# Seven weight units of each convolution mixer multiplied in three fp32r products instead of one fp32 product

## The chip, the cores and the metric

One core of a Trainium2 chip runs the whole kernel in one launch. The metric is the device time of one execution in microseconds (us). The kernel before takes 1773.08 us, the median of three executions (1772.91 to 1773.47).

Engines are called PE (TensorE, the matrix engine), DVE (VectorE), ACT (ScalarE), POOL (GpSimd) and SP (SyncE, which here only issues DMAs).

## The reference

The reference is a stack of six layers over 256 tokens of width 1024. The change touches only the layer that occurs twice in the first half, the conformer convolution mixer. Cut to what matters:

```python
def conformer_conv_mixer(h, w_in, conv_w, conv_b, ln_g, ln_b, w_out):   # h: 256 x 1024, w_in: 1024 x 6144
    proj = h @ w_in
    val, glu_gate, z = jnp.split(proj, 3, axis=-1)                      # 2048 channels each
    u = val * jax.nn.sigmoid(glu_gate)
    u = causal_depthwise_conv(u, conv_w) + conv_b                       # 31 taps
    u = jax.nn.silu(layer_norm(u, ln_g, ln_b))                          # over the 2048 channels
    return (u * jax.nn.silu(z)) @ w_out

# order of layers: conformer (a0), forgetting attention (b), short convolution (c), conformer (a1),
# then twice: a token mixer (m0, m1) and a convolutional feed-forward net (f0, f1)
```

## The kernel before, in words

All inputs and outputs are fp32. The weights are streamed once, in 629 pieces of at most 128 partitions x 1024 elements (512 KB), in an order fixed by `plan` (L365). SP loads them in that order into a ring of six buffers (`raw`, NRAW). Piece i can be loaded only when piece i-6 has been released, and SP issues strictly in order (`load`, L422).

A piece is used in one of two ways.

- A **plain** piece is read by PE straight from `raw` as fp32 (`plain_unit`, L565): eight matmuls with a 128x128 weight and 256 columns, for each of which the trace has two records. The buffer is released when PE has finished the unit.
- A **split** piece is first cast by ACT into an upper part (`wh`, the copy L113, in `feed_act` L463), and DVE then writes the rest, raw minus upper part, into `wl` (the subtraction L120, in `feed_dve` L475; called the low below). PE then does three fp32r matmuls for each of the eight weights, 24 in all (`unit`, L515). The `raw` buffer is released when the cast and the low are done, before PE has used them. `wh` and `wl` are rings of five.

A unit is one piece of 128 output channels. In a conformer layer (`plan_a`, L202; one program per engine: `pe_a` L844, `act_a` L922, `dve_a` L1057, `pool_a` L1197) the 2048 channels are taken in eight pairs of units p = 0 to 7. For each p PE multiplies the gate units g{p}.0 and g{p}.1, then the value units v{p}.0 and v{p}.1, and at p = 2, 4 and 6 one unit of z. Before the change all g are plain, v0.0, v0.1 and every v{p}.1 are plain, and v1.0 to v7.0 are split. The z units 0 to 7 (z0 to z3) are plain, the others split.

From p on, the work goes like this:

1. ACT takes the sigmoid of g{p} (`gate`).
2. DVE multiplies it by the value pair (`val(p)`: TENSOR_TENSOR `B<-ps,tmp` 128x512). This needs v{p}.1 from PE.
3. The convolution of pair p has 31 taps. ACT makes the first two. DVE adds 17 or 18 into PSUM, each as two SCALAR_TENSOR_TENSOR (`ps<-B,C,ps`). The other 12 or 11 are scaled by ACT into a ring of three `tmp` buffers (ACTIVATE `tmp<-B,C`), and POOL adds each into SBUF by two TENSOR_TENSOR. The nested functions `item` and `items` give each engine its taps in one common order: `items(p, a, b)` runs places a to b-1 of 30.
4. `conv_end(p)` on DVE (TENSOR_TENSOR `B<-ps,B`) joins the two sums. ACT squares the result (`stats`), and PE sums it over channels (`stats(q)`, MATMUL `ps<-B,C` and `ps<-tmp,C`).

POOL has waits of its own (`let_low`, L1202): from place 21 of pair p on it waits until DVE has finished the low of v{p+2}.0.

After p = 7 PE goes through the remaining z units with stats(5), (6) and (7) between them, then the 16 pieces of the output projection. PE, ACT, DVE and POOL each run their program strictly in order. In a1, PE, ACT and DVE also carry steps of a bias table for a later layer.

Of the kernel before, what the change touches and what calls it, by code (L numbers as in the profile page):

```python
# [18 lines left out]
E = 2048  # L19
# [9 lines left out]
PLAIN_Z = 4  # L29
# [164 lines left out]
def tiles(name, layer, c0, n=128, kt=8):  # L194
    return [(name, layer, 128 * k, 128, c0, n) for k in range(kt)]
# [6 lines left out]
def plan_a(j):  # L202
    A, out = f"a{j}", []

    def two(kind, p, base, *how):
        for n in range(2):
            out.append((f"{A}.{kind}{p}.{n}", tiles("a_w_in", j, base + p * 256 + 128 * n), how[n]))

    def z_unit(x):
        return [(f"{A}.z{x // 2}.{x % 2}", tiles("a_w_in", j, 2 * E + x * 128), "plain" if x < 2 * PLAIN_Z else "split")]  # L210

    for p in range(8):
        two("g", p, E, "plain", "plain")
        two("v", p, 0, "split" if p else "plain", "plain")
        if p in EARLY_Z:
            out += z_unit(EARLY_Z.index(p))
    for x in range(len(EARLY_Z), 16):
        out += z_unit(x)
    for k in range(16):
        out.append((f"{A}.o{k}", [("a_w_out", j, 128 * k, 128, 0, D)], "split"))  # L220
    return out
# [154 lines left out]
class Net:  # L376
# [467 lines left out]
    def pe_a(self, pe, j):  # L844
        s, A = self.s, f"a{j}"
        XN = self.xn()
        if j == 0:
            self.pe_bias(pe, 0, 7)
        self.pe_entry(pe, A, self.xnt)
        bank, prior = self.a_order()  # L850
        U, V, Z = self.a_views()

        def pair(kind, p, units=(0, 1)):
            b = self.ps[bank[kind, p]]
            if j == 0 and p == 0 and kind == "z":
                pe.wait_ge(*s["evac"]["bias", 0])
            if (kind, p) in prior:
                k, q = prior[kind, p]
                pe.wait_ge(*(s["conv"] if k == "v" else s["evac"])[A, k, q])
            for n in units:  # L860
                o = b[:, n * T:n * T + T]
                if kind == "g" or (kind == "v" and (p == 0 or n == 1)) or (kind == "z" and p < PLAIN_Z):
                    self.plain_unit(pe, o, f"{A}.{kind}{p}.{n}", XN, A)
                else:
                    self.unit(pe, o, f"{A}.{kind}{p}.{n}", A)

        def stats(q):


            pe.wait_ge(*s["conv"][A, "done", q])  # L870
            pe.wait_ge(*s["square"][A, q])
            x = [V[:, 2 * q, :], V[:, 2 * q + 1, :], self.tmp[5][:, 0:T], self.tmp[5][:, T:2 * T]]
            for g in range(4):
                ins = pe.matmul(self.ps[2][32 * g:32 * g + 32, 0:T], self.c("ones", 0, 32), x[g], start=q == 0,
                                stop=q == 7)
            ins.then_inc(s["sums"].up((A, q)), 1)

        def table(p):
            if j and 1 <= p <= 5:
                self.pe_bias_turn(pe, p, 3)  # L880

        for p in range(8):
            pair("g", p)
            if j == 0 and p == 0:
                self.pe_bias_turn(pe, 0, 7)
            table(p)
            if p >= 3:
                stats(p - 3)
            pair("v", p)
            if j and p < 5:  # L890
                self.pe_bias(pe, p + 1, 3)
            if p in EARLY_Z:
                x = EARLY_Z.index(p)
                pair("z", x // 2, (x % 2,))
        pair("z", 1, (1,))
        stats(5)
        pair("z", 2)
        pair("z", 3, (0,))
        stats(6)
        pair("z", 3, (1,))  # L900
        pair("z", 4)
        pair("z", 5, (0,))
        stats(7)
        pair("z", 5, (1,))
        pe.wait_ge(*s["evac"][A, "S"])
        if j:
            pe.wait_ge(*s["evac"]["bias", 5])
        for b in range(2):
            ins = pe.matmul(self.ps[3][:, b:4:2], self.tmp[4][:, 128 * b:128 * b + 128], self.c("which", 0, 2), start=True,
                            stop=True)  # L910
        ins.then_inc(s["sums"].up((A, "tokens")), 1)
        pair("z", 6, (0,))
        pe.wait_ge(*s["norm"][(A, "m"), "root"])
        pe.wait_ge(*s["evac"][A, "z", 1])
        self.spread(pe, 7, self.m["sm"][:, 112:116], (A, "m"))
        pair("z", 6, (1,))
        pair("z", 7)
        for k in range(15):
            self.pe_out(pe, A, k, 16)
        self.pe_out_last(pe, A, [15])  # L920

    def act_a(self, act, j):  # L922
# [43 lines left out]
        def items(p, a, b):  # L966
            for n in range(a, b):
                item(p, n)
# [22 lines left out]
        self.feed_act(act, f"{A}.v1.0", 1)  # L991
        for p in range(8):
            items(p, 0, 4)
            if p == 7:
                self.feed_act(act, f"{A}.z4.1", 0)
            if j and p < 5:
                self.act_bias_out(act, p + 1, 3)
            items(p, 4, 10)
            if p < 7:
                gate(p + 1)  # L1000
                if j and p < 5:
                    self.act_bias(act, p + 1, 3)
            else:
                self.feed_act(act, f"{A}.z5.0", 0)
                silu_z(1)
            items(p, 10, 14)
            if p < 6:
                self.feed_act(act, f"{A}.v{p + 2}.0", 0)
            if p == 4:
                silu_z(0)  # L1010
            items(p, 14, 18)
            if p:
                stats(p - 1)
            if p == 7:
                self.feed_act(act, f"{A}.z5.1", 0)
            items(p, 18, 22)
            if p >= 6:
                self.feed_act(act, f"{A}.z4.0" if p == 6 else f"{A}.z6.0", 0)
            if p == 7:
                silu_z(2)  # L1020
            items(p, 22, 30)
# [35 lines left out]
    def dve_a(self, dve, j):  # L1057
# [37 lines left out]
        def conv_end(p):  # L1095
            o = V[:, 2 * p:2 * p + 2, :].rearrange("p a t -> p (a t)")
            for i in (2 * p, 2 * p + 1):
                dve.wait_ge(*s["conv"][A, "tap", i, steps[i]])
            dve.wait_ge(*s["poolconv"][A, 2 * sum(self.pool_taps(x) for x in range(p + 1)) - 1])
            dve.tt(o, self.ps[p % 2], o, ALU.add).then_inc(s["conv"].up((A, "done", p)), 1)  # L1100
# [12 lines left out]
        for p in range(8):  # L1113
            items(p, 0, 8)
            if p:
                conv_end(p - 1)
            if p == 7:
                self.feed_dve(dve, f"{A}.z4.1", 0)
            items(p, 8, 14)
            if p == 7:  # L1120
                self.feed_dve(dve, f"{A}.z5.0", 0)
            items(p, 14, 20)
            if p < 7:
                val(p + 1)
            if p < 6:
                self.feed_dve(dve, f"{A}.v{p + 2}.0", 0)
            if p == 7:
                self.feed_dve(dve, f"{A}.z5.1", 0)
            items(p, 20, 28)
            if p >= 6:  # L1130
                self.feed_dve(dve, f"{A}.z4.0" if p == 6 else f"{A}.z6.0", 0)
            items(p, 28, 30)
# [64 lines left out]
    def pool_a(self, pool, j):  # L1197
        s, A = self.s, f"a{j}"
        U, V, Z = self.a_views()
        n = 0  # L1200

        def let_low(p, item):  # L1202

            names = [f"v{p + 2}.0" if item >= 21 and p < 6 else None]
            if p == 7:
                names = [u for at, u in ((9, "z4.1"), (15, "z5.0"), (21, "z5.1")) if item >= at]
            for u in names:
                if u is not None:
                    pool.wait_ge(*s["low"][self.at[f"{A}.{u}"]])

        for p in range(8):
            before = {2 * p: None, 2 * p + 1: None}
            for item, k in enumerate(self.taps(p), 1):
                if k >= self.pool_taps(p):
                    continue
                let_low(p, item)
                sh, q = 30 - k, self.tmp[2 + n % 3]
                for i in (2 * p, 2 * p + 1):
                    h = (i % 2) * T
                    pool.wait_ge(*s["tap"][A, i, k])  # L1220
                    if before[i] is not None:
                        pool.wait_ge(*s["poolconv"][A, "t", i, before[i]])
                    pool.tt(V[:, i, sh:T], V[:, i, sh:T], q[:, h + sh:h + T], ALU.add).then_inc(
                        s["poolconv"].up((A, "t", i, k), (A, 2 * n + i % 2)), 1)
                    before[i] = k
                n += 1
# [1690 lines left out]
```

## Time and profile before

| | |
|---|---|
| three executions | 1772.91, 1773.08, 1773.47 us |
| the profiled execution, its own time | 1773.47 us |
| its span (first to last instruction) | 1771.7 us |
| PE busy | 1726.1 us (97%), clock 0.994 of full speed |
| DVE, ACT, POOL busy | 1454.9 us (82%), 1082.4 us (61%), 291.8 us (16%) |
| PE, fp32r with `XS,wh` / `XS,wl` | 3600 matmuls / 2120 matmuls |
| PE, plain fp32 (`B,raw`) | 1056 records, 235.5 us |
| DVE, the lows (`wl<-raw,wh`) | 467, mean 1242 ns |
| ACT, the casts (`wh<-raw`) | 467, mean 1045 ns |

The shares are averages over stages that differ. Layer a0 stands between 14 and 227 us of the span, layer a1 between 746 and about 965 us. The convolution loops, which the change touches, are a part of each. In the timelines a row is a run of like instructions, with its start, its length, their number, and in brackets how long the engine had been idle before and what ended it. Rows of neighbours overlap slightly: an instruction's length includes the part that runs beside its successor.

### The profile page before, as it was taken

Reading aid. Unit: us, or ns where it says so; the run is one execution under the profiler, and the core shown is the slowest. Engines: PE = TensorE matmul, PEld = TensorE weight load, DVE = VectorE, ACT = ScalarE, POOL = GpSimd, SP = SyncE. Lnnn points to the kernel's source line nnn. Section 1 sums busy time; section 2 is a strip of 40 time slices with the busy share of each in tenths; the row PEclk is TensorE's granted clock in tenths of the full one; section 3 lists DMA queues with packets and bytes.
Section 4 is the critical chain, followed back from the end, with each engine's and each line's share of the span. In section 5 each row is a group of like instructions: output and inputs, shape, how many; then the busy total and the mean of one; then the engine's idle time right before and its main releaser. Section 6 shows DMA issues by size and latency. Waiting matters only on the chain.

```text
span 1771.7 us, 29474 instructions
## 1 busy us (share of the span) xinstructions
PE 1726.1 (97%) x10858; PEld 1530.7 (86%) x10858; DVE 1454.9 (82%) x2797; ACT 1082.4 (61%) x2101; POOL 291.8 (16%) x396
## 2 busy tenths in 40 slices
PE   7999999999999999999999999999999999999997
PEld 6888888888889999988888989988888998988885
DVE  6998878877788888779977698779987688789887
ACT  6887665655464444478875556576566556566664
POOL 2996000000000000068930000002000200002000
PEclk9999999999999999999999999999999999999998
DMA  6554568855568888644455664546774544546662
GB/s 224 154 163 159 168 217 306 266 183 178 183 211 290 289 291 295 215 143 143 143 179 167 202 202 121 173 147 190 243 230 157 167 145 129 176 139 189 222 191 71
DMA packets 92735, 339.53 MB, mean 192 GB/s; under 512 B 10288, under 2 KB 10672, under 8 KB 91952
## 3 DMA queue, kind: packets, MB, share of 16 engines
q1 hardware_dynamic: 92592, 337.64, 58.3%
q8 instruction: 87, 1.43, 0.3%
q14 instruction: 56, 0.46, 0.1%
HBM read 336.55 MB, written 1.05 MB: 191 GB/s over the span
## 4 chain that ended last, share of the span: by engine, by line
PE 79%; DVE 12%; ACT 7%; issue 1%; DMA 1%; SPq 0%; ACTq 0%; DVEq 0%
PE ps L104 78%; DVE wl L120 4%; ACT tmp L110 3%; ACT wh L113 2%; PE ps L107 2%; DVE tmp L130 1%; DVE raw L130 1%; DVE tmp L120 1%; DVE sm L142 1%; ACT os L113 1%; DVE tmp L125 1%; DVE B L120 0%; DVE os L120 0%; DMA raw<-in_w 0%; DVE sc L151 0%
## 5 line engine op out<-in xcount | busy, mean ns | idle before, releaser
L104 PE MATMUL ps<-XS,wh 128*128 128x256 f32 (+1 forms) x3600 | 773.3, 306 | 9.1 <-DVE wl L120 4.9
L120 DVE TENSOR_TENSOR wl<-raw,wh 128x1024 fp32r<-128x1024 f32 x467 | 571.8, 1242 | 107.6 <-ACT wh L113 105.5
L104 PEld LDWEIGHTS ps<-XS,wh 128*128 128x128 f32 x3600 | 577.3, 190 | 48.8 <-issue 18.5
L104 PE MATMUL ps<-XS,wl 128*128 128x256 f32 x2120 | 583.7, 281 | 0.0
L113 ACT CAST wh<-raw 128x1024 fp32r<-128x1024 f32 x467 | 473.9, 1045 | 154.2 <-PE ps L104 140.3
L104 PEld LDWEIGHTS ps<-XS,wl 128*128 128x128 f32 x2120 | 403.1, 190 | 6.6
L120 POOL TENSOR_TENSOR B<-B,tmp 128x236 f32<-128x236 f32 (+11 forms) x368 | 249.6, 717 | 652.9 <-ACT tmp L110 641.4
L104 PE MATMUL ps<-wh,os 128*128 128x512 f32 x864 | 280.7, 393 | 3.1 <-DVE B L133 2.1
L104 PE MATMUL ps<-B,raw 128*128 128x256 f32 x1056 | 235.5, 383 | 0.0
L104 PEld LDWEIGHTS ps<-B,raw 128*128 128x128 f32 x1056 | 200.4, 192 | 31.0 <-issue 4.4
L130 DVE SCALAR_TENSOR_TENSOR ps<-B,C,ps 128x253 f32<-128x253 f32 (+17 forms) x560 | 216.9, 475 | 3.8 <-ACT ps L110 3.8
L104 PEld LDWEIGHTS ps<-wh,os 128*128 128x128 f32 x864 | 163.1, 189 | 36.6 <-issue 3.8
L104 PE MATMUL ps<-wh,XS 128*128 128x512 f32 x576 | 179.5, 391 | 0.0
L104 PE MATMUL ps<-wl,os 128*128 128x512 f32 x432 | 169.0, 391 | 0.0
L110 ACT ACTIVATE tmp<-B,C 128x236 f32<-128x236 f32 (+11 forms) x368 | 151.4, 477 | 25.3 <-POOL B L120 24.6
L120 POOL TENSOR_TENSOR X<-X,B 128x512 f32<-128x512 f32 x24 | 42.1, 1753 | 701.9 <-PE ps L104 701.9
L110 ACT ACTIVATE B<-ps 128x256 f32<-128x256 f32 (+2 forms) x156 | 72.9, 480 | 117.4 <-PE ps L104 117.1
L104 PEld LDWEIGHTS ps<-wh,XS 128*128 128x128 f32 x576 | 107.2, 188 | 21.5
L110 ACT ACTIVATE tmp<-ps 128x128 f32<-128x128 f32 (+3 forms) x178 | 73.3, 427 | 80.5 <-PE ps L104 64.0
L130 DVE SCALAR_TENSOR_TENSOR raw<-raw,cb 128x1024 f32<-128x1024 f32 x96 | 116.5, 1219 | 0.0
L104 PE MATMUL ps<-wl,XS 128*128 128x512 f32 x288 | 112.3, 390 | 0.0
L104 PEld LDWEIGHTS ps<-wl,os 128*128 128x128 f32 x432 | 81.6, 189 | 16.2
(162 smaller groups left out, 1636.6 us busy)
## 6 DMA issues: line engine op xcount, KB each, us to landing
raw<-in_w SPq DMA_DIRECT2D x628, 512.0 KB, 4.4
B<-in_ln SPq DMA_DIRECT2D x4, 1024.0 KB, 6.6
C<-in_cst SPq DMA_DIRECT2D x1, 1103.5 KB, 9.9
X<-in_x SPq DMA_DIRECT2D x2, 512.0 KB, 5.7
out_x<-X SPq DMA_DIRECT2D x4, 256.0 KB, 2.5
cb<-in_cb SPq DMA_DIRECT2D x1, 512.0 KB, 12.9
pos<-in_pos SPq DMA_DIRECT2D x1, 160.0 KB, 2.3
raw<-in_w SPq DMA_DIRECT2D x1, 128.0 KB, 2.0
```

The costliest lines, as they stand in the source:

```text
L104: return NOTHING if self.e is None else self.e.matmul(*a, **k)
L107: return NOTHING if self.e is None else self.e.transpose(*a)
L110: return NOTHING if self.e is None else self.e.activation(*a, **k)
L113: return NOTHING if self.e is None else self.e.copy(*a)
L120: return NOTHING if self.e is None else self.e.tensor_tensor(o, a, b, op)
L125: return self.e.tensor_scalar(o, a, s1, s2, op0) if op1 is None else self.e.tensor_scalar(o, a, s1, s2, op0, op1)
L130: return self.e.scalar_tensor_tensor(out=o, in0=a, scalar=s, in1=b, op0=op0, op1=op1, **k)
L142: return NOTHING if self.e is None else self.e.tensor_reduce(o, a, AX, ALU.max)
```

## The change

The seven units v1.1 to v7.1 of each conformer layer become split instead of plain, 14 units in all. So ACT casts and DVE subtracts for them, in places given by hand:

- v1.1 right after v1.0, ahead of the loop (by the lookahead of 1 that stands there already);
- v{p+1}.1, for p = 1 to 6, on ACT after place 3 of pair p, and on DVE after conv_end(p-1), which follows place 7 of pair p;
- POOL waits, from place 9 of pair p on, for that low.

```diff
-    def two(kind, p, base, *how):
+    def two(kind, p, base, how):
         for n in range(2):
-            out.append((f"{A}.{kind}{p}.{n}", tiles("a_w_in", j, base + p * 256 + 128 * n), how[n]))
+            out.append((f"{A}.{kind}{p}.{n}", tiles("a_w_in", j, base + p * 256 + 128 * n), how))
...
-        two("g", p, E, "plain", "plain")
-        two("v", p, 0, "split" if p else "plain", "plain")
+        two("g", p, E, "plain")
+        two("v", p, 0, "split" if p else "plain")
...
-                if kind == "g" or (kind == "v" and (p == 0 or n == 1)) or (kind == "z" and p < PLAIN_Z):
+                if kind == "g" or (kind, p) == ("v", 0) or (kind == "z" and p < PLAIN_Z):
                     self.plain_unit(pe, o, f"{A}.{kind}{p}.{n}", XN, A)
...                                                     # act_a
             items(p, 0, 4)
+            if 1 <= p < 7:
+                self.feed_act(act, f"{A}.v{p + 1}.1", 0)
...                                                     # dve_a
             if p:
                 conv_end(p - 1)
+            if 1 <= p < 7:
+                self.feed_dve(dve, f"{A}.v{p + 1}.1", 0)
...                                                     # pool_a, let_low
-            names = [f"v{p + 2}.0" if item >= 21 and p < 6 else None]
+            names = [f"v{p + 1}.1" if item >= 9 and 1 <= p < 7 else None, f"v{p + 2}.0" if item >= 21 and p < 6 else None]
```

On DVE, in a0, this is what now stands at p = 1, behind conv_end(0) (`B<-ps,B`). Each tap is a SCALAR_TENSOR_TENSOR; x2 is one tap for the two units of a pair:

```order
 L130 SCALAR_TENSOR_TENSOR ps<-B,C,ps 128x251 x2
 L120 TENSOR_TENSOR B<-ps,B 128x512
+L120 TENSOR_TENSOR wl<-raw,wh 128x1024
 L130 SCALAR_TENSOR_TENSOR ps<-B,C,ps 128x250 x2
 L130 SCALAR_TENSOR_TENSOR ps<-B,C,ps 128x249 x2
```

One low (of v2.1) has come in; the same stands at p = 2 to 6 and in a1, nothing else moves on DVE there.

On ACT, at the start of pair p = 1 of a0, the cast comes in behind the first tap that is meant for POOL. The casts write to the ring `wh`; the taps write to the ring tmp2, tmp3, tmp4:

```order
 L110 ACTIVATE B1<-B3,C 128x256 x2
 L110 ACTIVATE tmp2<-B3,C 128x236 x2
+L113 CAST wh1<-raw5 128x1024
 L110 ACTIVATE tmp3<-B3,C 128x235 x2
 L110 ACTIVATE tmp4<-B3,C 128x234 x2
```

Every later tap that ACT makes for POOL stands one cast further back.

On SP, the loads behind those of pairs p = 4 to 7 and of the plain z units of a0, each with what it waits for. Before:

```order
L154 DMA raw<-in_w 128x1024 [waits s_gemm] x3
L154 DMA raw<-in_w 128x1024 [waits s_low,s_cast]
L154 DMA raw<-in_w 128x1024 [waits s_gemm] x4
L154 DMA raw<-in_w 128x1024 [waits s_low,s_cast]
L154 DMA raw<-in_w 128x1024 [waits s_gemm] x6
```

And now:

```order
L154 DMA raw<-in_w 128x1024 [waits s_gemm] x2
L154 DMA raw<-in_w 128x1024 [waits s_low,s_cast] x2
L154 DMA raw<-in_w 128x1024 [waits s_gemm] x3
L154 DMA raw<-in_w 128x1024 [waits s_low,s_cast] x2
L154 DMA raw<-in_w 128x1024 [waits s_gemm] x5
```

A buffer that held v{p}.1 is now released by its cast and low instead of by PE's matmuls. The load that follows v7.1 in its buffer is that of z4.0, the first split unit of z.

## Rows read from the trace of the kernel before

**Rows 1.** Two windows: PE, PEld, DVE, ACT, POOL busy us (instructions), PEclk, DMA.

```profile
30.00:138.00 108.00, 108.00 (x600) 94.43 (x599) 104.11 (x251) 91.69 (x220) 98.74 (x154) 1.00 0.50 153
752.00:875.00 123.00, 123.00 (x716) 104.53 (x715) 105.60 (x253) 97.08 (x232) 101.04 (x154) 1.00 0.47 144
```

**Rows 2.** Chain of waits, a0: start us, us, what.

```profile
117.89 18.11 PE ps L104 x99
...
136.02 3.73 DMA raw<-in_w
```

**Rows 3.** Timeline of PE, a0: start us, us, instructions, idle before.

```profile
38.78 10.53 PE L104 MATMUL ps<-B,raw 128*128 128x256 f32 x48
...
154.06 0.41 PE L104 MATMUL ps<-B,C 128*32 128x256 f32 x2 [3.49 <-ACT tmp L110]
...
154.86 5.13 PE L104 MATMUL ps<-B,raw 128*128 128x256 f32 x16
159.64 0.59 PE L104 MATMUL ps<-XS,wh 128*128 128x256 f32 x2
...
168.55 0.41 PE L104 MATMUL ps<-B,C 128*32 128x256 f32 x2
```

**Rows 4.** Timeline of DVE, a0.

```profile
42.44 0.69 DVE L120 TENSOR_TENSOR B<-ps,tmp 128x512 f32<-128x512 f32 x1 [2.60 <-PE ps L104]
43.04 1.22 DVE L120 TENSOR_TENSOR wl<-raw,wh 128x1024 fp32r<-128x1024 f32 x1
44.18 7.71 DVE L130 SCALAR_TENSOR_TENSOR ps<-B,C,ps 128x243 f32<-128x243 f32 x20
...
52.38 6.21 DVE L130 SCALAR_TENSOR_TENSOR ps<-B,C,ps 128x250 f32<-128x250 f32 x16
58.48 0.70 DVE L120 TENSOR_TENSOR B<-ps,tmp 128x512 f32<-128x512 f32 x1
...
137.98 0.69 DVE L120 TENSOR_TENSOR B<-ps,tmp 128x512 f32<-128x512 f32 x1
...
165.03 0.69 DVE L120 TENSOR_TENSOR B<-ps,B 128x512 f32<-128x512 f32 x1 [1.18 <-POOL B L120]
```

**Rows 5.** Groups by form, DVE, 42.4 to 138 us: busy us, mean ns.

```profile
L120 DVE TENSOR_TENSOR wl<-raw,wh 128x1024 fp32r<-128x1024 f32 x6 | 8.9, 1479 | 0.0
```

**Rows 6.** The same for 775.5 to 862 us.

```profile
L120 DVE TENSOR_TENSOR wl<-raw,wh 128x1024 fp32r<-128x1024 f32 x6 | 8.2, 1370 | 0.0
```

**Rows 7.** DVE's waits, 776 to 875 us: total us, times, longest.

```profile
DVE B L120 <- PE ps L104: 4.9, 2, 2.8
```

**Rows 8.** Timeline of DVE, a1.

```profile
775.00 0.69 DVE L120 TENSOR_TENSOR B<-ps,tmp 128x512 f32<-128x512 f32 x1 [4.00 <-PE ps L104]
...
859.48 2.03 DVE L120 TENSOR_TENSOR wl<-raw,wh 128x1024 fp32r<-128x1024 f32 x1
...
874.97 0.69 DVE L120 TENSOR_TENSOR B<-ps,tmp 128x512 f32<-128x512 f32 x1
```

**Rows 9.** Timeline of POOL, a0 and a1.

```profile
124.59 15.31 POOL L120 TENSOR_TENSOR B<-B,tmp 128x228 f32<-128x228 f32 x24 [1.16 <-DVE wl L120]
...
861.59 15.30 POOL L120 TENSOR_TENSOR B<-B,tmp 128x228 f32<-128x228 f32 x24 [1.17 <-DVE wl L120]
```

**Rows 10.** Timeline of ACT, a0 and a1.

```profile
139.78 1.04 ACT L113 CAST wh<-raw 128x1024 fp32r<-128x1024 f32 x1 [2.76 <-DMA raw<-in_w]
...
142.99 0.15 ACT L110 ACTIVATE ps<-C 128x1 f32<-128x1 f32 x1
...
877.73 1.04 ACT L113 CAST wh<-raw 128x1024 fp32r<-128x1024 f32 x1 [3.72 <-DMA raw<-in_w]
...
880.95 0.15 ACT L110 ACTIVATE ps<-C 128x1 f32<-128x1 f32 x1
```

**Rows 11.** Timeline of PE after the stage between.

```profile
392.95 0.48 PE L104 MATMUL ps<-wh,os 128*128 128x512 f32 x1 [2.09 <-DVE B L133]
```

**Rows 12.** The window after it: busy us by engine, PEclk, DMA.

```profile
394.00:396.00 2.00, 2.00 (x6) 1.52 (x5) 0.89 (x1) 0.00 (x0) 0.00 (x0) 0.50 0.61 131
```

## The prediction, made before the changed kernel ran

> **What bounds the kernel now.** I read the busy time by windows first, then the chain of waits through layer a0, then the timelines of the four engines, side by side, for a0 and a1. The windows [rows 1] show two full engines. In a0's loop, 30 to 138 us, PE is busy 108 of 108 us, and DVE 104.1 with its only pauses at the start; POOL has 98.7 and ACT 91.7. In a1 PE is again full (123 of 123), while DVE has 105.6. So whatever a change takes from PE there, it must not hand to DVE.
>
> The chain in a0 [rows 2] runs on PE until 136.02, when v7.1 and with it its buffer is done. It then goes through the load of z4.0 into that buffer (3.73 us) and ACT's cast of it. From there it runs along ACT to the square for stats(6), which PE has waited 3.49 us for at 154.06 [rows 3]. After that PE runs on without a gap into the output projection. So the time of a layer hangs on when stats(6) can start.
>
> On DVE [rows 4] val(1) waits 2.60 us for PE at 42.44. After that no row has an idle time up to val(7) at 137.98, 95.54 us later. In a1 the same stretch takes from 775.00 to 874.97 [rows 8], 99.97 us, of which 4.9 us in two pieces are waits for PE [rows 7]. DVE's own work in it is 95.1 us. In a0 DVE sets the pace of the loop with PE just ahead of it; in a1 PE is in front in half of the pairs.
>
> **What PE gains.** Three plain units take 10.53 us [rows 3], 3.5 each. Three split units (z4.0, z4.1, z5.0) lie between 159.64 and 168.55 [rows 3], 2.97 each. So PE saves 0.5 to 0.6 us a unit, 14 x 0.55 = 7.7 us in both layers, if PE is what everything waits for. Only v1.1 is surely such a place: val(1) waits for it in both layers, and its low is made before val(0), where DVE in a1 is idle. I take -0.6 us for it in each layer.
>
> **What DVE pays.** Six lows per layer come between conv_end(p-1) and place 8 of pair p. A low is shown as 1.22 us, and 43.04 to 44.18 is 1.14 to the next start [rows 4]; the shown length holds 0.08 of overlap. The six lows in a0's loop average 1479 ns, the six in a1's 1370 [rows 5, 6]. Without the overlap that is 1.40 and 1.29 us. The longest is 2.03 [rows 8], so 1.95. The long ones are those that begin while POOL is adding. The new lows fall where POOL is in the midst of its adds, like most old ones, so I take these means; the bounds are 1.14 and 1.95.
>
> The Trainium skill (SBUF — State Buffer, section "SBUF: two separate sides") says that DVE, with two SBUF inputs, and GpSimd take a shared port pair as an exclusive lock for a whole instruction. By that rule a low would begin up to one POOL add late, and POOL would stand still during every low. The rows agree: POOL's runs of 24 begin with a wait of 1.16 us for a low [rows 9]. A run is 15.31 us, 0.64 an add, so a low that finds POOL in an add would cost up to 1.14 + 0.64 = 1.8 us by the rule; six of them make 10.7 us, inside my bounds.
>
> **POOL** loses about 1.16 us more per pair, as much as DVE. Its 24 adds (22 in every second pair) are 15.3 and 14.0 us. With two such waits that is 17.0 us a pair on average. DVE's pair becomes 15.9 + 1.4 = 17.3. So POOL keeps up, with little to spare. **ACT** pays six casts of about 1 us. It is busy 91.7 of 108 us [rows 1], and its cast comes some 2 us before DVE wants it; but its next tap for POOL is one cast later. I cost this at nothing; if POOL waits for it in each pair, some 0.5 us a pair are added.
>
> **When PE waits.** The new v{p+1}.1 can't start before its low. In p = 1 that ends at 52.38 + 1.4 - 0.6 = 53.2 us, and PE, done with v2.0 at about 51.3, waits 1.9. From the low to val(p+1) DVE has 14 or 16 taps before it, 58.48 - 52.38 = 6.1 us for 16 and 5.4 for 14 [rows 4]. PE's unit of 2.9 us fits in twice over. So these waits, up to 3.5 us each in a0 as DVE falls back, cost nothing by themselves. They only mean that PE's saving is not used. If PE's clock falls to half behind one of them, the unit takes up to 5.8 us, which fits 16 taps and just misses 14.
>
> **Sum for a0.** val(7) comes -0.6 + 6 x 1.40 = +7.8 us later, at 145.8. The low of v7.1 is done 14 taps earlier, at 140.4, and releases the buffer. The load takes 3.73 us, to 144.1. ACT wants z4.0 at 139.78 - 2.76 = 137.02, now + 7.8 = 144.8 [rows 10]. So ACT's wait for this DMA goes. What is late next is POOL: ACT's last tap of p = 6 needs the add with which POOL's run ends, 124.59 + 15.31 = 139.90 [rows 9], and with 0.8 us for the tap ACT would start pair 7 at 140.8 instead of 142.99 [rows 10]. The gain is 2.2 us, not 2.76. stats(6) moves by +7.8 - 2.2 = +5.6 us, to 159.7. PE arrives there at: 140.4 + 2.9 for v7.1, then 14.5 us as before (136.02 to 154.06 less 3.49), so 157.8, and waits 1.9 us. Behind it stats(7) must not be late. conv_end(7) is at 165.03 now, 1.18 us of that for POOL [rows 4]; DVE gets there at 163.85 + 7.8 = 171.7. Add 1.4 us for it and the square: 173.1, and PE comes at 168.55 + 5.6 = 174.2 [rows 3]. It holds by 1.1 us.
>
> **Sum for a1.** DVE has 95.1 + 6 x 1.29 = 102.8 us of work from val(1), which starts at 775.0 - 0.6 = 774.4. So val(7) is at 877.2 instead of 874.97, +2.2: most of the new lows fill what were waits for PE. PE, now 0.55 us a unit faster, is not in front any more. ACT starts pair 7 at 880.95; without the wait of 3.72 us for the DMA it would be POOL's end, 861.59 + 15.30 + 0.8 = 877.7 [rows 9, 10], 3.2 us earlier. stats(6) moves by 2.2 - 3.2 = -1.0 us.
>
> **Total:** +5.6 - 1.0 = +4.6 us. Between a0 and a1 and behind a1 nothing is changed, and PE is the engine that runs through there, so both shifts are carried to the end. The profiled execution took 1773.47 us (span 1771.7 and 1.8 around it), which makes 1778.1. It is the slowest of the three; against the median of 1773.08 the forecast is 1777.7 us.
>
> **Bounds.** With lows of 1.14 us a0 has -0.6 + 6.8 - 2.2 = +4.0, a1 1.3 - 3.2 = -1.9, together +2.1. PE's clock may add a gain: the unit after the 3.49 us wait took 5.13 us instead of 3.5 [rows 3], and after a wait of 2.09 us the granted clock was 0.50 too [rows 11, 12], the lower of the two levels (1.2 of 2.4 GHz). The new waits for stats(6) are 1.9 us, so I count on no gain (nearest row 2.09). If the clock stays up it is up to 1.3 us a layer: +2.1 - 2.6 = -0.5, or 1772.6. With lows of 1.95 us it is +8.9 and +2.9, together +11.8: 1784.9.
>
> **Rivals.**
> - *PE is the bound, and it is faster.* PE is full in both loops [rows 1]. Then all 14 units pay, -7.7 us: 1765. Against it: in a0 DVE has no idle time from 42 to 138 us, and each of its pairs gets longer. A half of it could hold in a1, where DVE waits 4.9 us: with clean lows, the DMA wait gone and the clock up the two layers reach -0.5 us, not -3.5. I give 0.10 to faster.
> - *The new waits and the freed buffer balance.* Clean lows (1.14) and a clock that stays up, or PE's waits shorter than I think: +0 to +3 us, 1773 to 1776. For it: the first low in a0 is 1.14 [rows 4], and without the one of 2.03 the other five in a1 average (8.2 - 2.03) / 5 = 1.23, overlap included [rows 6, 8]. 0.25.
> - *POOL or ACT becomes the bound of the loop (slower by more).* POOL's adds and two waits come to 17.0 us a pair, and ACT's tap one cast later adds up to 0.5 us, 17.5 against DVE's 17.3. Then ACT, which waits for POOL's ring of three, doesn't get its 2.2 and 3.2 us back: 4.6 + 5.4 = +10.0, 1783. It decides as soon as POOL's pair is over 17.3 us. 0.20.
> - My forecast, +3 to +8 us: 0.45.
>
> Within 0.2% (3.5 us) this kernel's time can't be told from no change. The forecast of +4.6 lies a little over that. Slower by over 0.2% holds most of my own case and all of the POOL case, 0.65; within 0.2% gets 0.25, faster 0.10. The range leaves out the PE case and the far end of the slow ones: 1771 to 1785.
>
> **What would show it.** In the profile after, val(2) to val(7) in a0 stand 16.7 to 17.8 us apart (now 15.3 to 16.4), with one more `wl` row in each pair, and DVE without idle time from val(1) on. The PE rows have a wait for DVE `wl` before the second value unit of each pair in a0, at most 4 us; in a1 short ones or none. ACT has no wait for `raw<-in_w` before the cast of z4.0 in either layer. PE's wait for ACT before stats(6) is about 2 us. PE's busy time falls by some 7 us while the span grows. It is wrong if a0's DVE still shows 95 us from val(1) to val(7), which would mean that the lows found a gap, or if the stretch from stats(6) to the projection grows, which would mean that stats(7) or a z low is late.

## The result, and the profile after

The changed kernel takes 1783.69 us (median of four executions, 1781.24 to 1784.35), the kernel before 1773.28 in the same series. Over all nine executions on record (1781.24 to 1785.77) the ratio is 1.0055, interval 1.0042 to 1.0069. By the medians that is 10.4 us slower, by the ratio 9.8, where 4.6 were forecast. The profiled execution took 1785.77 us (span 1783.9), 12.3 more than that of before.

The page, busy us of each engine over the span:

```profile
PE 1725.5 (97%) x10970; PEld 1534.5 (86%) x10970; DVE 1480.0 (83%) x2811; ACT 1095.5 (61%) x2115; POOL 298.0 (17%) x396
```

Fourteen units are now cheaper on PE, and still its busy time is the same to 0.6 us. What went up is DVE, by 25 us. Two windows, one for the loop of each layer, show why [rows 1]; the columns are as there:

```profile
43.00:147.00 104.00, 96.16 (x580) 85.28 (x579) 103.73 (x235) 87.11 (x201) 92.33 (x139) 0.97 0.44 137
783.00:886.00 103.00, 98.58 (x631) 85.39 (x628) 102.14 (x232) 88.29 (x205) 95.57 (x136) 0.98 0.43 139
```

DVE is now the full engine in both layers, 103.7 of 104 us and 102.1 of 103. PE has 8 and 4 us of holes, and its granted clock is 0.97 and 0.98 instead of 1.00. So its work is less, but part of it runs at the lower level (0.57 in the window 88 to 96 us, 0.70 in 826 to 831). The lower level in these two windows costs about 0.03 x 104 + 0.02 x 103 = 5 us of PE time, an estimate, and takes up most of the 7 us by which PE's busy time was to fall.

The chain of waits through the same loop in a0 (start us, us, what), which ran on PE before [rows 2]:

```profile
43.10 0.69 DVE B L120
43.79 1.36 DVE wl L120
45.15 3.84 DVE ps L130 x11
...
52.77 0.59 DVE B L120
53.37 1.27 DVE wl L120
54.63 5.43 DVE ps L130 x15
...
147.54 3.77 DVE ps L130 x10
151.31 0.16 DVE wl L120
151.47 3.95 issue
155.42 3.94 DVE ps L130 x10
```

Each pair has two lows (`wl`), as forecast. The new thing is at the end, in pair 7: a low that begins at 151.31 is followed by 3.95 us of "issue". The timeline of DVE shows it as one long instruction, the low of z4.0, in a0 and in a1 (start us, us, instructions, idle before):

```profile
52.69 0.68 DVE L120 TENSOR_TENSOR B<-ps,B 128x512 f32<-128x512 f32 x1
53.29 1.34 DVE L120 TENSOR_TENSOR wl<-raw,wh 128x1024 fp32r<-128x1024 f32 x1
...
146.86 0.68 DVE L120 TENSOR_TENSOR B<-ps,tmp 128x512 f32<-128x512 f32 x1
147.47 3.84 DVE L130 SCALAR_TENSOR_TENSOR ps<-B,C,ps 128x243 f32<-128x243 f32 x10
151.22 4.27 DVE L120 TENSOR_TENSOR wl<-raw,wh 128x1024 fp32r<-128x1024 f32 x1
155.42 3.94 DVE L130 SCALAR_TENSOR_TENSOR ps<-B,C,ps 128x238 f32<-128x238 f32 x10
...
891.22 4.28 DVE L120 TENSOR_TENSOR wl<-raw,wh 128x1024 fp32r<-128x1024 f32 x1
```

From val(1), at 43.10 in the chain, to val(7) it is 103.76 us in a0 (95.54 before [rows 4]) and 104.51 in a1 (99.97 [rows 8]). The new low of pair 1 takes 1.34 us. The one of z4.0 takes 4.27 and 4.28; the longest of all others in these layers is 2.36. In the kernel before it was this:

```profile
142.33 1.33 DVE L120 TENSOR_TENSOR wl<-raw,wh 128x1024 fp32r<-128x1024 f32 x1
```

What POOL does in that time, after:

```profile
141.67 16.29 POOL L120 TENSOR_TENSOR B<-B,tmp 128x234 f32<-128x234 f32 x24 [1.65 <-DVE wl L120]
```

And before:

```profile
141.29 9.62 POOL L120 TENSOR_TENSOR B<-B,tmp 128x228 f32<-128x228 f32 x12 [1.39 <-ACT tmp L110]
```

Before, POOL idled 1.39 us for ACT, which was held up by the load of z4.0, and then did 12 adds in 9.62 us. One could read 0.80 us an add into this, and gaps between them; but record by record each add starts about 0.04 us before the last one ends, as after the change. Ten of them take about 0.67 us, and two take 1.65 and 1.67, because a low runs beside each. The first of the two, in the window 142.6 to 144.1 us:

```profile
L120 POOL TENSOR_TENSOR B<-B,tmp 128x227 f32<-128x227 f32 x1 | 1.6, 1649 | 0.0
```

The low at 142.33 began 0.25 us before the end of an add, got in at that end, and held up the next one. (In a1 before, the low began at 879.32, just after POOL had come out of an idle time of 2.35 us, and took 1.22 us.) After the change the low begins at 151.22, together with an add of POOL, and waits for this add and four more, to 154.41. So POOL's adds are no closer than before. What is new is that this low did not get in at the end of the first add. ACT is no longer held up there, and low and adds meet at another moment.

PE in the same places [rows 3] (timeline, start us, us, idle before); the first four rows are of a0, the last three of a1:

```profile
89.21 0.77 PE L104 MATMUL ps<-XS,wh 128*128 128x256 f32 x2 [3.43 <-DVE wl L120]
...
161.92 0.41 PE L104 MATMUL ps<-B,C 128*32 128x256 f32 x2 [2.50 <-DVE ps L130]
...
162.49 5.41 PE L104 MATMUL ps<-B,raw 128*128 128x256 f32 x16
...
176.88 0.41 PE L104 MATMUL ps<-B,C 128*32 128x256 f32 x2 [0.36 <-ACT tmp L110]
...
901.85 0.41 PE L104 MATMUL ps<-B,C 128*32 128x256 f32 x2 [2.41 <-ACT tmp L110]
...
902.41 3.72 PE L104 MATMUL ps<-B,raw 128*128 128x256 f32 x16
...
916.92 0.41 PE L104 MATMUL ps<-B,C 128*32 128x256 f32 x2 [2.15 <-ACT tmp L110]
```

Two kinds of waits are new. PE waits for a low five times in a0 (7.8 us together, the longest shown), which costs nothing by itself. And in a1 stats(7) at 916.92 is 2.15 us late; before, PE came there without a wait. The windows of 40 us behind stats(6) show the granted clock, the last but two of the columns, at 0.96 in both layers of the kernel after:

```profile
162.00:202.00 40.00, 39.64 (x275) 36.22 (x275) 33.73 (x64) 26.87 (x46) 11.46 (x15) 0.96 0.54 176
902.00:942.00 40.00, 37.85 (x268) 35.20 (x262) 32.58 (x62) 25.16 (x43) 11.48 (x15) 0.96 0.54 175
```

It was 0.96 before as well, so the change loses nothing there by the clock:

```profile
154.00:194.00 40.00, 39.94 (x276) 36.45 (x277) 30.62 (x58) 27.13 (x46) 10.89 (x14) 0.96 0.52 172
892.00:932.00 40.00, 39.99 (x278) 36.35 (x279) 30.27 (x56) 27.34 (x46) 10.91 (x14) 0.96 0.52 172
```

In a0 it fell behind the wait for stats(6), where 16 records took 5.41 us. In a1 these took 3.72, the time at the higher level (2.4 GHz), so it fell later, behind the wait for stats(7).

ACT in a0: the cast of z4.0, without the wait of 2.76 us [rows 10], its start of pair 7, and the cast of z5.0:

```profile
146.39 1.03 ACT L113 CAST wh<-raw 128x1024 fp32r<-128x1024 f32 x1
...
150.19 0.15 ACT L110 ACTIVATE ps<-C 128x1 f32<-128x1 f32 x1
...
153.85 1.63 ACT L110 ACTIVATE tmp<-B,C 128x235 f32<-128x235 f32 x4
156.04 1.05 ACT L113 CAST wh<-raw 128x1024 fp32r<-128x1024 f32 x1 [0.55 <-DMA raw<-in_w]
```

With this the two layers can be accounted for by stretch. a0 begins at PE's first x64 run of plain matmuls (22.09 us before, 23.34 after), a1 at the 16 short matmuls just ahead of that run (744.55 and 752.48). Each ends where PE starts the next layer. The column e1 is the first experiment below. Differences to before, us:

| stretch | before | forecast | after | e1 |
|---|---|---|---|---|
| a0: start to val(1) | 20.35 | -0.6 | -0.59 | -0.58 |
| val(1) to val(7) | 95.54 | +8.4 | +8.22 | +7.57 |
| val(7) to stats(6) | 16.08 | -2.2 | -1.02 | -1.05 |
| stats(6) to layer b | 77.94 | 0 | +0.46 | -1.64 |
| a1: start to val(1) | 30.45 | -0.6 | -0.58 | -0.59 |
| val(1) to val(7) | 99.97 | +2.8 | +4.54 | +3.93 |
| val(7) to stats(6) | 17.04 | -3.2 | -2.05 | -1.95 |
| stats(6) to layer m0 | 78.38 | 0 | +2.29 | -1.43 |
| sum | | +4.6 | +11.3 | +4.3 |

The profile of after also starts its first layer 1.25 us later than that of before. Experiments 3, 5 and 7 have it at 23.76, 23.13 and 23.36 us, 7 with a time like that of before, so I take it for spread.

### The profile page after: what moved, and what is told of

The parts are those of the page before. It is cut to its first block, busy times and chain, and to the rows that moved or that the text cites. A ratio compares the mean times of both kernels' runs of the same rounds, so it can differ in the third digit from the quotient of the medians.

```text
span 1783.9 us, 29766 instructions
## 1 busy us (share of the span) xinstructions
PE 1725.5 (97%) x10970; PEld 1534.5 (86%) x10970; DVE 1480.0 (83%) x2811; ACT 1095.5 (61%) x2115; POOL 298.0 (17%) x396
## 3 DMA queue, kind: packets, MB, share of 16 engines
HBM read 336.55 MB, written 1.05 MB: 189 GB/s over the span
## 4 chain that ended last, share of the span: by engine, by line
PE 69%; DVE 21%; ACT 7%; issue 2%; POOL 0%; DMA 0%; SPq 0%; ACTq 0%; DVEq 0%; POOLq 0%
PE ps L104 68%; DVE ps L130 7%; DVE wl L120 6%; ACT tmp L110 3%; ACT wh L113 2%; PE ps L107 2%; DVE B L120 1%; DVE tmp L130 1%; DVE raw L130 1%; DVE tmp L120 1%; DVE sm L142 1%; ACT os L113 1%; DVE tmp L125 1%; DVE os L120 0%; POOL B L120 0%
## 5 line engine op out<-in xcount | busy, mean ns | idle before, releaser
L104 PE MATMUL ps<-XS,wh 128*128 128x256 f32 (+2 forms) x3824 | 818.7, 306 | 18.3 <-DVE wl L120 14.1
L120 DVE TENSOR_TENSOR wl<-raw,wh 128x1024 fp32r<-128x1024 f32 x481 | 597.1, 1258 | 105.1 <-ACT wh L113 103.0
L104 PEld LDWEIGHTS ps<-XS,wh 128*128 128x128 f32 (+1 forms) x3824 | 615.8, 192 | 59.5 <-issue 29.3
L104 PE MATMUL ps<-XS,wl 128*128 128x256 f32 x2232 | 617.5, 282 | 0.0
L113 ACT CAST wh<-raw 128x1024 fp32r<-128x1024 f32 x481 | 488.1, 1044 | 145.1 <-PE ps L104 141.3
L104 PEld LDWEIGHTS ps<-XS,wl 128*128 128x128 f32 x2232 | 426.7, 191 | 6.6
L120 POOL TENSOR_TENSOR B<-B,tmp 128x236 f32<-128x236 f32 (+11 forms) x368 | 254.8, 730 | 659.8 <-ACT tmp L110 637.1
L104 PE MATMUL ps<-B,raw 128*128 128x256 f32 x832 | 186.8, 384 | 0.0
L104 PEld LDWEIGHTS ps<-B,raw 128*128 128x128 f32 x832 | 158.5, 193 | 24.9 <-issue 3.3
## 6 DMA issues: line engine op xcount, KB each, us to landing
C<-in_cst SPq DMA_DIRECT2D x1, 1103.5 KB, 10.4
```

The lines of the kernel that those rows point to most:

```text
L104: return NOTHING if self.e is None else self.e.matmul(*a, **k)
L113: return NOTHING if self.e is None else self.e.copy(*a)
L120: return NOTHING if self.e is None else self.e.tensor_tensor(o, a, b, op)
```

## The experiments

My theory: DVE's added lows are the price (near 5 us), and the rest of the 10.4 is the low of z4.0, shut out by POOL's adds. The rivals: POOL's new waits cost it, or PE's later clock, or the change costs by itself whatever z4.0 does. Later the question was whether the freed buffer or PE's saving can be had for less. All are compared with the kernel before on the same chip, at 1773.8 to 1774.4 us in these series. The executions of one kernel differ, and with them the granted clock. In experiment 4 the four executions with a granted clock of 0.996 took 1772.65 to 1773.14 us, those with 0.992 and 0.993 took 1777.88 to 1779.24. Several use a set `SECOND` of (layer, pair), which says for which v{p}.1 the change is made:

```diff
-        two("v", p, 0, "split" if p else "plain")
+        two("v", p, 0, "split" if p else "plain", "split" if (j, p) in SECOND else "plain")
...                                  # and in act_a, dve_a and let_low
-            if 1 <= p < 7:
+            if 1 <= p < 7 and (j, p + 1) in SECOND:
```

**1. POOL waits for z4.0's low.** The changed kernel, and in `let_low`:

```diff
+            if p == 6 and item >= 27:
+                names.append("z4.0")
```

> The changed kernel, and POOL also waits, from place 27 of pair 6 on, until DVE has finished the low of z4.0. Theory A (starved low): in the changed kernel the low of z4.0 is shown as 4.3 us in both layers instead of 1.3 because POOL's adds run back to back through it; this is on the path to stats(6). Then the row falls to 1.2 to 1.7 us, conv_end(6) comes 2.6 to 3 us earlier in each layer, and the time goes from 1783.7 to 1777 to 1780. Theory B (the long row is only overlap, the loss is the six lows in the loop alone): the row may shorten but the time stays at 1783 to 1785.

Measured: 1778.5 us (six executions), ratio 1.0033 (1.0021 to 1.0045). Its DVE timeline, a0:

```profile
145.79 0.67 DVE L120 TENSOR_TENSOR B<-ps,tmp 128x512 f32<-128x512 f32 x1
...
150.15 1.21 DVE L120 TENSOR_TENSOR wl<-raw,wh 128x1024 fp32r<-128x1024 f32 x1
...
155.13 0.67 DVE L120 TENSOR_TENSOR B<-ps,B 128x512 f32<-128x512 f32 x1
```

The low is 1.21 us again (1.75 in a1), and conv_end(6) comes 9.34 us after val(7) instead of 12.41. By the medians one wait on POOL takes back 5.2 us of the 10.4; by the ratios it is 3.9 of 9.8, and the two intervals just touch (1.0042 and 1.0045). So two fifths to a half of the slowdown was this one instruction per layer. The table shows by which way: stats(6) itself moves by little (0.7 and 0.5 us), but behind it the loss is 2.1 and 3.7 us. PE there:

```profile
160.82 0.41 PE L104 MATMUL ps<-B,C 128*32 128x256 f32 x2 [2.49 <-ACT tmp L110]
...
161.39 3.72 PE L104 MATMUL ps<-B,raw 128*128 128x256 f32 x16
```

stats(7) is not waited for any more in either layer, and the granted clock stays up:

```profile
162.00:202.00 40.00, 40.00 (x280) 37.04 (x279) 33.58 (x61) 27.36 (x48) 9.72 (x12) 1.00 0.57 185
```

**2. Meant to leave out the added lows.** A test of the units' names in my edit matched none of them, so all lows were still made; what ran is the changed kernel without POOL's new waits, and the expectation speaks of a kernel that did not run:

```diff
-            names = [f"v{p + 1}.1" if item >= 9 and 1 <= p < 7 else None, f"v{p + 2}.0" if item >= 21 and p < 6 else None]
+            names = [f"v{p + 2}.0" if item >= 21 and p < 6 else None]
```

> The changed kernel without the seven added lows of each layer (and without POOL's waits for them): ACT casts, PE does its three products with the upper part in place of the rest, so the small term of these units is left out. Theory A (DVE's lows are the price): val(1) to val(7) in a0 is back at 95 to 96 us and in a1 at 95 to 97, ACT's wait for the DMA of z4.0 is gone, and the kernel is faster than before: 1764 to 1769. Rival C (ACT's casts in front of POOL's taps, or PE's extra waits, are the price): the loop stays at 99 us or more in a0 and the time is 1774 or more.

Measured: 1790.63 us (1781.48 to 1799.79), ratio 1.009 (1.0064 to 1.0117). The miss shows something all the same. Its timeline in a0, POOL, DVE and PE:

```profile
62.09 14.04 POOL L120 TENSOR_TENSOR B<-B,tmp 128x228 f32<-128x228 f32 x22 [1.16 <-DVE wl L120]
...
70.13 7.08 DVE L120 TENSOR_TENSOR wl<-raw,wh 128x1024 fp32r<-128x1024 f32 x1
...
77.35 0.76 PE L104 MATMUL ps<-XS,wh 128*128 128x256 f32 x2 [6.10 <-DVE wl L120]
```

POOL's run of 22 adds ends at 62.09 + 14.04 = 76.13, and the low of v3.1, which should have begun at 70.13, ends at 77.21, 1.08 us behind that. It waited for the whole rest of the run, and PE 6.1 us for it. But it need not happen. In the same execution the low of v5.1 began just as long (0.30 us) before the end of an add, amid adds just as close, and got in at that end; POOL's add behind it is the long one. DVE, and POOL in the window 110.3 to 111.7 us:

```profile
109.93 1.39 DVE L120 TENSOR_TENSOR wl<-raw,wh 128x1024 fp32r<-128x1024 f32 x1
...
L120 POOL TENSOR_TENSOR B<-B,tmp 128x234 f32<-128x234 f32 x1 | 1.7, 1665 | 0.0
```

The six executions lie far apart. The fastest is as fast as the changed kernel's fastest, which would fit a number of shut-out lows that changes from one to the next; only one execution was profiled. So POOL's waits in `let_low` are no cost to be saved but what bounds the time of a low.

**3 and 4. One layer alone**: `SECOND` holds v1.1 to v7.1 of a0, or of a1.

> The change in layer a0 alone. Theory A: a0 carries 7 of the 10 us: 1779 to 1781.5, val(1) to val(7) in a0 103 to 104 us, z4.0's low 4.3 us there and 1.2 in a1. Theory D (a1 is where it is lost, since its PE and ACT carry the bias table as well): 1776 or less.

> The change in layer a1 alone. Theory A: a1 costs 3 to 4.5 us, of which 3 are z4.0's low: 1776 to 1778. My forecast for a1 (-1 us, without the starved low) would give 1772 to 1773. The shares of this run and of the one with a0 alone should add up to the whole, 10.4 us.

Measured: a0 alone 1780.36 us, ratio 1.0035 (1.0023 to 1.0047); a1 alone 1776.39, 1.0010 (1.0001 to 1.0018). That is +6.5 and +2.6 us, together 9.1 of the 10.4. The low of z4.0 follows the change: with a0 changed it is 4.29 us there and 1.21 in a1; with a1 changed it is 4.29 in a1. The layers add up within the spread, and a0, where DVE had no idle time, pays more, as forecast. The 2.6 us of a1 are the weaker number: the four executions with the highest granted clock were as fast as the kernel before.

**5. The added lows left out.** The kernel of 1, but DVE makes no low for v1.1 to v7.1, POOL waits for none, and PE multiplies these units with `wh` in place of `wl`. So the small term of the product is left out and the upper product is added twice; PE's and ACT's work is kept. Left out is each low together with POOL's wait for it, but experiment 2 shows that leaving out these waits alone gains nothing.

```diff
+    def no_low(self, i):
+        n = self.pieces[i][0]
+        return n[0] == "a" and n[3] == "v" and n[4] != "0" and n.endswith(".1")
...                                  # feed_dve
+            if self.kind[i] == "split" and self.no_low(i):
+                continue
```

> The changed kernel with POOL's wait for z4.0, and without the seven added lows of each layer and POOL's waits for them: ACT casts, PE does its three products with the upper part in place of the rest, so the small term of these units is left out. Theory A (the added lows on DVE are what the loop pays): val(1) to val(7) is 95 to 96 us in a0 and 95 to 97 in a1, the DMA wait before z4.0's cast is gone, stats(6) comes 2 to 4 us earlier than before in each layer, and the time is 1764 to 1769. Rival C (ACT's casts ahead of POOL's taps, or PE's new waits, are the price): the loops stay over 99 us in a0 and the time is 1773 or more.

Measured: 1768.41 us (1768.25 to 1768.8), ratio 0.9963 (0.9951 to 0.9976): 6.0 us faster than before, where 1 is 4.7 slower. Its lengths from val(1) to val(7) are 95.49 us in a0, the same as before, and 98.79 in a1. So the added lows are what makes the change slower, and PE's saving is there: 6.0 us, near the 7.7 of the forecast's PE rival. DVE's work in the loop takes it away. In a0 this kernel gains 2.0 us and in a1 4.3. In a0 DVE sets the pace even so; in a1 the granted clock also stayed at 1.00 over the 40 us behind stats(6), which was 0.96 before and is worth some 1.6 us. (The low of z4.0 was 2.26 and 2.90 us here in spite of the wait: POOL had still two and three adds to do before the place at which it waits.)

**6 to 8. Only the units at the ends of the loop**, where a low is cheap (v1.1's falls before val(0)) or buys something (v7.1's frees the buffer of z4.0). 6 is v1.1 and v7.1 in both layers with the wait of 1; 7 is v7.1 alone with it; 8 is v1.1 alone without it.

```diff
+SECOND = {(j, p) for j in range(2) for p in (1, 7)}     # 6; 7: (0, 7), (1, 7); 8: (0, 1), (1, 1)
```

> Only v1.1 and v7.1 of each layer are split, and POOL waits for z4.0's low. Theory A: v1.1 gains 0.6 us where DVE waits for PE; v7.1 costs one low (1.2 to 1.5 us in a0, less in a1 where DVE has waits) and releases z4.0's buffer early, worth 2.2 us in a0 and 3.2 in a1. Sum -1.5 to -2.8 in a0 and -3 to -4 in a1: 1767 to 1770, faster than both kernels. Rival E (stats(7) or POOL's end takes over at once, so the freed buffer is worth nothing): 1772.5 to 1775.

> Only v7.1 of each layer is split, and POOL waits for z4.0's low. Theory A: as the run with v1.1 and v7.1 but without the 0.6 us of v1.1 in each layer: 1768 to 1771. Rival E: 1773 to 1776.

> Only v1.1 of each layer is split; nothing else is changed. Theory A: val(1) comes 0.6 us earlier in each layer, and since the chain of waits runs on PE up to v7.1, the whole gains 0.5 to 1.2 us: 1772 to 1773. Rival F (the early low and cast delay val(0) and POOL, so nothing is gained): 1773.5 to 1774.5.

Measured: 1773.85, 1772.98 and 1773.44 us, against 1774.41: ratios 0.9996 (0.9987 to 1.0004), 0.9993 (0.9984 to 1.0002), 0.9995 (0.9986 to 1.0003). None can be told from no change, where 6 was expected at 1767 to 1770. In 6 ACT has no wait for z4.0, but 0.68 and 1.31 us for the load of z5.0 (0 before). The waits for the load after that one, 2.26 and 2.34 us, are hardly longer than before (2.24 and 2.10). So the freed buffer hands a part of its wait on to the next load.

**9 to 11. Four units of a1, one unit of a1, and the wait alone.**

```diff
+SECOND = {(1, 1), (1, 3), (1, 5), (1, 7)}               # 9; 10: (1, 7); 11: none. All with the wait of 1
```

> Layer a0 as before; in a1 only v1.1, v3.1, v5.1 and v7.1 are split, and POOL waits for z4.0's low. v1.1, v3.1 and v5.1 are the units for which DVE waited for PE in the kernel before (4.0, 2.1 and 2.8 us). Theory A (a low costs nothing where DVE would wait for PE, and full price elsewhere): val(1) to val(7) in a1 is 98 to 99.5 us, stats(6) comes 3 to 4 us earlier, a1 gains 3 to 4.5 us: 1769.5 to 1771.5. Rival E (the freed buffer and the loop gain nothing, since z5.0's load or stats(7) takes over): 1773 to 1775.

> Layer a0 as before; in a1 only v7.1 is split, and POOL waits for z4.0's low. The run with v7.1 in both layers gained 2.3 us in a1 by the marks in its profile and nothing in a0. Theory A: 1771 to 1772.5, of which the low of v7.1 takes back about 1.2 us of what the buffer gives. Rival E: 1773 to 1775.

> The kernel before with POOL's wait for z4.0's low alone, no further unit split. Theory A (that wait helps only where POOL has adds in hand while DVE wants the low; in the kernel before POOL was idle for 1.4 us there): 1773 to 1775, no difference that can be measured, z4.0's low 1.2 us in both layers. Rival G (the wait by itself speeds up or slows down the stage): more than 2 us away from before.

Measured: 1773.97, 1773.78 and 1773.88 us against 1773.87: ratios 1.0000 (0.9991 to 1.0009), 0.9998 (0.9989 to 1.0006) and 1.0001 (0.9992 to 1.0010). The wait alone does nothing, so 1 repaired what the change had broken and not a fault of before. 9 was to use a1's 4.9 us of idle DVE time [rows 7] and missed. From val(1) to val(7) it took 100.87 us, 0.9 more than before. Its PE and ACT:

```profile
891.17 0.41 PE L105 MATMUL ps<-B,C 128*32 128x256 f32 x2 [3.49 <-ACT tmp L111]
...
891.74 5.41 PE L105 MATMUL ps<-B,raw 128*128 128x256 f32 x16
```

```profile
885.29 1.05 ACT L114 CAST wh<-raw 128x1024 fp32r<-128x1024 f32 x1 [1.56 <-DMA raw<-in_w]
...
900.84 1.05 ACT L114 CAST wh<-raw 128x1024 fp32r<-128x1024 f32 x1 [2.34 <-DMA raw<-in_w]
```

The wait of 3.72 us for z4.0's load [rows 10] is gone; in its place z5.0 is waited for 1.56 us, and PE, which comes earlier, waits 3.49 us for stats(6) and runs the next 16 records at the lower level (5.41 us). The second wait, 2.34 us, was 2.10 before. No version with all products beats the kernel before by an amount that can be measured.

## Why the prediction was right, and where its size was off

It was right on direction (slower), on the range (1771 to 1785) and on the reason. Its steps, against the table:

- **v1.1 gains 0.6 us a layer.** Measured 0.58 to 0.59, four times.
- **Six lows in a0 cost 8.4 us.** 8.22 measured, 7.57 in 1. The new ones were 1.21 to 1.62 us (mean 1.32, 1.24 without the overlap), under my 1.40; the old low of pair 6 was 2.02. DVE is without idle time from val(1) on.
- **In a1 2.8 us.** 4.5 measured, 3.9 in 1. Too small: I took all of DVE's 4.9 us of waiting as room for lows. A wait for PE is left there (0.8 us at 852.48), and the twelve lows average 1.43 us, not 1.29 + 0.08.
- **The freed buffer gives 2.2 and 3.2 us.** Only 1.0 and 2.0. (139.90 + 0.8 is 140.7 and not 140.8, so the sum should have had 2.3.) The wait for z4.0 went, but ACT reached pair 7 not 2.2 but 1.7 us earlier in a0 (150.19 - 146.86 = 3.33 behind val(7), 5.01 before), and then waited 0.55 us for z5.0, whose load I had not followed.
- **Nothing behind stats(6).** This is where it failed. The prediction had: "Behind it stats(7) must not be late", and then "It holds by 1.1 us." It did not: 0.36 us late in a0, 2.15 in a1. The sum for conv_end(7) there had the low of z4.0 at its length of before. It took 3 us more, and in experiment 1, without these 3 us, stats(7) is in time. In a0 that is all of it: from stats(6) to stats(7) it is 14.96 us after and 12.86 in 1, which is the whole difference of 2.1 us between the two columns. The chain of waits runs on DVE there up to conv_end(7), so the fall of the clock behind stats(6) cost nothing more. In a1 it is 15.07 and 12.85, and the other 1.5 us of the 3.7 lie behind stats(7), where the clock fell (0.66 in the window 917 to 922 us).
- **PE's busy time falls by some 7 us** (a sign it named). It fell by 0.6: PE ran part of both loops at the lower level, as shown above.

That low is the mis-sized term. I priced the six new lows with bounds of 1.14 and 1.95 us, and moved the old ones at their old lengths. I had worked out that ACT's wait goes and that ACT and POOL then run closer, and did not ask how this low would meet POOL's adds. Its length was 4.27 us, outside the bound of 1.8 us that the prediction took for a low that finds POOL in an add. One sign was also misread: the 1.16 us in [rows 9] are POOL's own wait for the low in `let_low`. The row that shows DVE holding up POOL is the add of 1649 ns above.

The POOL rival (+10.0 us, 1783) met the time but not the way: POOL waits for lows 10.8 us in a0's loop and ACT still had its gain. It didn't decide the pace; it shut DVE out at one place.

With the low repaired, kernel 1 is 4.7 us over before by the medians (5.9 by the ratio), and 4.6 was forecast. The table says that this is partly luck. Against its column e1 the forecast is 3.5 us too low on three stretches (1.1 and 1.2 from val(7) to stats(6), 1.1 in a1's loop) and 0.8 us too high in a0's loop. It is also 3.1 us too high behind stats(6): that is the clock, whose gain of "up to 1.3 us a layer" I had put in the bounds and not in the sum. PE's waits for stats(6) were 2.49 and 2.53 us in 1, against 3.49 and 3.29 before, and the 16 records behind them took 3.72 instead of 5.13 and 4.70.

Two things stay open. Why the low of z4.0 missed the end of the first add, where most lows get in (last section), no profile tells; that a wait on POOL's side repairs it is shown. And the clock: it fell behind waits of 2.50 us (after, a0), 2.51 (experiment 10), 2.55 (7, a0) and 2.61 (6, a0), where the 16 records took 5.41 us. It didn't behind 2.49 and 2.53 (1), 2.55 (5, a1), 2.60 (3, a0) and 2.65 (2, a0), where they took 3.72. So the length of the wait alone does not decide it.

## What to carry to other kernels

Moving work from an engine that is full to one that is also full gained nothing here; look for the engine without idle time in the loop, and let it pay nothing (experiment 5: 6.0 us faster where the change is 10.4 slower). When a change removes a wait, follow every engine behind it: with ACT's wait for a DMA gone, an old DVE instruction met POOL's adds at another moment and took 3 us more. Where an instruction of DVE with both inputs in SBUF runs beside a busy POOL and the critical path goes through it, try a wait on POOL's side just ahead of it (4.27 to 1.21 us and 4.28 to 1.75 here); where it was short anyway the wait did nothing (experiment 11). And don't read a mean length of a row as gaps between its instructions: one long instruction among short ones gives the same mean.

## What the runs showed of the hardware

A DVE subtraction with both inputs in SBUF and an add of POOL do not run at the same time. In most cases the low gets in at the end of the add in whose course it begins. In the layers a0 and a1 of all 13 profiles, counted record by record, this was so 146 times. POOL's adds were back to back there (each began 0.03 to 0.07 us before the last one ended), the low was shown as 1.20 to 1.70 us, and the next add was the long one. In 27 cases the low missed this first end, and then it got in at no later end of an add either (25 more went by) until POOL stopped: at a wait or the end of its run 21 times, at a short pause 6 times. Most of the 27 met a wait of POOL after one more add and are 1.75 to 2.3 us long. The costly ones are those of z4.0 (4.27, 4.28, 4.29 and 4.29 us in three kernels, 4.05 in a1 of experiment 2) and of v3.1 (7.08 us, in a0 of experiment 2). What decides between the two cases the profiles don't tell: in experiment 2 two lows that began 0.30 us before the end of an add went different ways.

The pause that let the low of z4.0 in, in a0 of the changed kernel: one add ended at 154.41 us and the next began at 154.42, where all others of the run began 0.04 to 0.05 before the last one ended. That next add is shown as 1623 ns, where others of its form take about 680, in the window 154.9 to 155.8:

```profile
L120 POOL TENSOR_TENSOR B<-B,tmp 128x235 f32<-128x235 f32 x1 | 1.6, 1623 | 0.0
```

ACT's next taps for POOL begin at 153.85 us, behind a cast, so POOL had run out of taps about there. In the four other lows that got in so, the next add also began late, from 0.01 us before to 0.04 after the last one's end (0.23 in one more). That the pause is what let them in is argued from this agreement, not tested.

The Trainium skill (SBUF — State Buffer, section "SBUF: two separate sides") says that whichever of the two starts first has the shared port pair for the whole instruction and the other blocks. By that rule the low would wait for one add at most, by an estimate 1.14 + 0.68 = 1.8 us, as the prediction had it. The 146 cases agree with it, and all cases agree that one blocks the other. The 27 do not agree with the bound: the low of z4.0 waited for five adds here and that of v3.1 for the rest of one and nine more in experiment 2.
